# Second block of a two-block model: gate steps moved, a pair of selection products, denominators over a sum of tiles, a pair of output tiles

## What is computed

```python
h = rms_norm_2(x, norm1_g)
z = h @ w_in + b_in                       # all branches' features and 4 x 1024 gates
# mLSTM, 4 heads of width 128; chunked in the reference, equal to the full causal form:
#   s_qk = (q k^T) * exp(decay[t, s] - m_t), causal
#   num = s_qk @ v ; den = sum over s of s_qk
#   h = num / max(|den|, exp(-m_t))
y_ml = rms_norm_2(mlstm(q, k, v, i, f), ml_norm_g) * sigmoid(mo)
y_fx = forgetting_attention(...)
# RG-LRU: r, i = sigmoid(block-diagonal products of xc)
#   a = exp(-8 r softplus(-lambda)); u = sqrt(1 - a^2) * (i * xc)
#   scan over time: h = a h + u ; y = h * gelu(ry)
y_lru = rg_lru_branch(...)
y_gla = gla(...)
ycat = stack([y_ml, y_fx, y_lru, y_gla])
yb = einsum('bsnw,nwd->bsnd', ycat, w_branch)
merged = sum(sigmoid(gates) * yb)
x = x + merged @ w_o
x = x + square(relu(rms_norm_2(x, norm2_g) @ w_up)) @ w_down
```

## Time and profile before

| | |
|---|---|
| median of 3 runs | 3535.67 us |
| the profiled execution, its own time | 3532.56 us |
| its span | 3530.8 us |
| TensorE busy | 97% of the span, 16646 matmul records |
| VectorE, ScalarE, GpSimd busy | 51%, 34%, 8% |
| TensorE's share of the chain that ended last | 92% |
| mean granted TensorE clock | 0.983 of full |

### The profile page before, as it was taken

The page is one execution under the profiler, slowest core; times in us unless marked ns, Lnnn a source line. Parts: engine busy times, 40 slices in busy tenths (PEclk is TensorE's granted clock), DMA queues, the critical chain, the costliest instruction groups (busy, mean ns, idle before and its releaser), DMA issues.

```text
span 3530.8 us, 40839 instructions
## 1 busy us (share of the span) xinstructions
PE 3435.0 (97%) x16646; PEld 2758.3 (78%) x16646; DVE 1786.8 (51%) x3100; ACT 1185.1 (34%) x1990; POOL 287.3 (8%) x238
## 2 busy tenths in 40 slices
PE   8999999999999999999899999999999999999999
PEld 6888786777888788887777878887788777878887
DVE  7666456565565733334654643334453655454433
ACT  3222236542222232223555332223321444223322
POOL 0000220002000200021200100013011000020000
PEclk9999999999999999999999999999999999999999
DMA  6565322123565523223210322322221223122232
GB/s 239 206 211 189 101 78 72 40 69 109 191 219 196 179 98 99 92 95 107 68 49 25 114 83 84 108 82 93 68 78 55 75 73 115 42 96 84 96 107 78
DMA packets 120218, 376.37 MB, mean 107 GB/s; under 512 B 13280, under 2 KB 28000, under 8 KB 120032
## 3 DMA queue, kind: packets, MB, share of 16 engines
q1 hardware_dynamic: 120032, 373.76, 31.8%
HBM read 371.61 MB, written 2.10 MB: 106 GB/s over the span
## 4 chain that ended last, share of the span: by engine, by line
PE 92%; DVE 4%; ACT 2%; issue 1%; POOL 1%; DMA 0%; SPq 0%; POOLq 0%; ACTq 0%; DVEq 0%
PE ps L445 26%; PE ps L446 26%; PE ps L447 26%; PE ps L660 2%; PE ps L683 2%; PE ps L554 2%; PE ps L488 1%; PE ps L495 1%; PE ps L479 1%; PE ps L481 1%; PE ps L480 1%; DVE s_wl L1429 1%; ACT s_wh L944 1%; POOL s_small L2109 0%; PE ps L521 0%
## 5 line engine op out<-in xcount | busy, mean ns | idle before, releaser
L445 PE MATMUL ps<-s_uh,s_wh 128*128 128x512 f32 x2824 | 1137.4, 403 | 30.2 <-DVE s_ul L1491 12.8
L1429 DVE TENSOR_TENSOR s_wl<-s_raw,s_wh 128x1024 fp32r<-128x1024 f32 (+3 forms) x645 | 707.1, 1097 | 845.2 <-ACT s_wh L944 843.0
L446 PE MATMUL ps<-s_uh,s_wl 128*128 128x512 f32 x2824 | 1111.1, 393 | 0.0
L447 PE MATMUL ps<-s_ul,s_wh 128*128 128x512 f32 x2824 | 1110.5, 393 | 0.0
L944 ACT ACTIVATE s_wh<-s_raw 128x1024 fp32r<-128x1024 f32 (+3 forms) x645 | 587.9, 913 | 727.6 <-PE ps L447 531.2
L445 PEld LDWEIGHTS ps<-s_uh,s_wh 128*128 128x128 f32 x2824 | 537.5, 190 | 173.1 <-issue 49.4
L447 PEld LDWEIGHTS ps<-s_ul,s_wh 128*128 128x128 f32 x2824 | 536.6, 190 | 115.1
L446 PEld LDWEIGHTS ps<-s_uh,s_wl 128*128 128x128 f32 x2824 | 537.9, 190 | 109.0 <-issue 2.4
L447 PE MATMUL ps<-s_fl,s_wh 128*128 128x512 f32 x960 | 378.2, 394 | 0.0
L445 PE MATMUL ps<-s_fh,s_wh 128*128 128x512 f32 x960 | 378.2, 394 | 0.0
L446 PE MATMUL ps<-s_fh,s_wl 128*128 128x512 f32 x960 | 378.2, 394 | 0.0
(11 more groups left out here) (401 smaller groups left out, 3374.1 us busy)
## 6 DMA issues: line engine op xcount, KB each, us to landing
s_raw<-w SPq DMA_DIRECT2D x616, 512.0 KB, 3.6
s_raw<-w SPq DMA_DIRECT2D x96, 192.0 KB, 2.4
s_raw<-w SPq DMA_DIRECT2D x64, 256.0 KB, 2.6
s_raw<-w SPq DMA_DIRECT2D x19, 128.0 KB, 2.0
s_x<-x SPq DMA_DIRECT2D x4, 512.0 KB, 6.3
out<-s_x SPq DMA_DIRECT2D x8, 256.0 KB, 2.2
s_raw<-w SPq DMA_DIRECT2D x4, 420.0 KB, 3.6
s_crow<-crow SPq DMA_DIRECT2D x2, 512.0 KB, 3.4
```

The lines of the kernel that those rows point to most:

```text
L445: TE.matmul(o, w_hi(i, k), h, start=first, stop=False)
L446: TE.matmul(o, w_lo(i, k), h, start=False, stop=False)
L447: return TE.matmul(o, w_hi(i, k), l, start=False, stop=last)
L1429: V.tensor_tensor(wl[w][:, 0:n], raw[t % NRAW][:, 0:n], wh[w][:, 0:n].bitcast(F32), SUB).then_inc(*s_lo.up(("lo", t)))
```

## The change

- mLSTM: four gate steps stand ahead of the transposes; the loop and `head_norm` keep theirs, so none is left for `merge(0)`.
- mLSTM: `lfm` lies at partitions 32 to 35, so that its selection product uses other rows of the array than that of `lmx`; both waits stand ahead of both products.
- mLSTM: the ones-product runs over the first 128 columns of `lE[0]`, and once over `lsum`, 384 columns, into which VectorE adds the four tiles. TensorE waits for the last addition; ScalarE waits for the additions before it overwrites `lE`; VectorE waits for the last `db` before it overwrites `lsum`.
- RG-LRU: two gate steps stand ahead of the products `ga` and `gx`; `merge(2)` has two fewer.
- Output: the first two `wo2` tiles are made by `fm_pair`.

```diff
@@ plan
-    for m in range(8):
+    pair("wo2", 0, "wo2", 1)
+    for m in range(2, 8):
         fm("wo2", 8, m)
@@ buffers
-            lai, lmx, lfm = (sb(d, n, [4, 512]) for n in ("lai", "lmx", "lfm"))
+            lai, lmx = (sb(d, n, [4, 512]) for n in ("lai", "lmx"))
+            lfm = sb(d, "lfm", [36, 512])[32:36, :]
+            lsum = sb(d, "lsum", [128, 384])
@@ tensor_engine, second
             c = Clock(0)
+            fill(c, 4)
             o = take(("acol",))
...
-                sel = col("sel", 128 * h, 128)[0:4, :]
+                sel = col("sel", 128 * h, 128)
                 mb, eb = take(("mb", h)), take(("eb", h))
                 pe.wait_ge(*s_dve["mx"])
-                TE.matmul(mb[:], sel, lmx[:], start=True, stop=True).then_inc(*s_pe.up(("ps", ("mb", h))))
                 pe.wait_ge(*s_dve["fmx"])
-                TE.matmul(eb[:], sel, lfm[:], start=True, stop=True).then_inc(*s_pe.up(("ps", ("eb", h))))
+                TE.matmul(mb[:], sel[0:4, :], lmx[:], start=True, stop=True).then_inc(*s_pe.up(("ps", ("mb", h))))
+                TE.matmul(eb[:], sel[32:36, :], lfm, start=True, stop=True).then_inc(*s_pe.up(("ps", ("eb", h))))
...
-                    TE.matmul(nb[:, 128 * j:512], lv[:, j, sl(h)], lE[j][:, 0:n], start=j == 0, stop=j == 3)
-                    TE.matmul(db[:, 128 * j:512], ones, lE[j][:, 0:n], start=j == 0, stop=j == 3).then_inc(
-                        *s_pe.up(("lE", h, j), *([("ps", ("nb", h)), ("ps", ("db", h))] if j == 3 else [])))
+                    ins = TE.matmul(nb[:, 128 * j:512], lv[:, j, sl(h)], lE[j][:, 0:n], start=j == 0, stop=j == 3)
+                    if j == 0:
+                        ins = TE.matmul(db[:, 0:128], ones, lE[0][:, 0:128], start=True, stop=True)
+                    ins.then_inc(*s_pe.up(("lE", h, j), *([("ps", ("nb", h))] if j == 3 else [])))
+                pe.wait_ge(*s_dve["lsum", h, 3])
+                TE.matmul(db[:, 128:512], ones, lsum[:], start=True, stop=True).then_inc(*s_pe.up(("ps", ("db", h))))
...
             c = Clock(2)
+            fill(c, 2)
...
-            for m in range(8):
+            fm_pair(("wo", "s", 0), "wo2", 0, ("wo", "s", 1), "wo2", 1, ("mu",))
+            for m in range(2, 8):
@@ scalar_engine, second
             c = Clock(0)
+            fill(c, 4)
...
                     if h:
                         act.wait_ge(*s_pe["lE", h - 1, j])
+                        act.wait_ge(*s_dve["lsum", h - 1, max(j, 1)])
...
             c = Clock(2)
+            fill(c, 2)
...
+            fm_pair("wo2", 0, "wo2", 1)
+            for m in range(2, 8):
@@ vector_engine, second
             V.tensor_tensor(lfm[:], lmx[:], ffx[0:4, :], ADD).then_inc(*s_dve.up("fmx"))
+            fill(c, 4)
             dve.wait_ge(*s_pe["ps", ("acol",)])
...
                     V.scalar_tensor_tensor(lE[j][:, 0:n], bank(g)[:, 0:n], 128.0 ** -0.5, lE[j][:, 0:n], MUL, MUL).then_inc(*s_dve.up(("mE", h, j), frees=g))
+                    if j:
+                        if j == 1 and h:
+                            dve.wait_ge(*s_pe["ps", ("db", h - 1)])
+                        dve.wait_ge(*s_dve.now())
+                        o = 128 * j - 128
+                        first = lE[0][:, 128:512] if j == 1 else lsum[:, o:384]
+                        V.tensor_tensor(lsum[:, o:384], first, lE[j][:, 0:n], ADD).then_inc(*s_dve.up(("lsum", h, j)))
...
             c = Clock(2)
+            step(c, 2)
...
+            fm_pair("wo2", 0, "wo2", 1)
             for m in range(8):
-                fm("wo2", 8, m)
+                if m > 1:
+                    fm("wo2", 8, m)
                 dve.wait_ge(*s_pool["fx", m])
                 update(("wo", "s", m), m, None, ("x", "up", m))
```

## The result

Over 20 runs each on the same chips, the changed kernel took 3532.98 us in the median (3525.47 to 3540.83) and the kernel before 3537.88 (3532.71 to 3542.83). The ratio is 0.9979, 95% interval 0.9972 to 0.9987: 7.4 us less, with 4.6 to 9.9 as bounds (the two medians alone are 4.9 apart). The forecast was 8.6 us less. The forecast of 3527.1 us was counted from a median of 3535.67; this series has the kernel before 2.2 us higher, and 3532.98 as such lies 1 us above the range.

A forecast was written before the change was run, and what follows sets the result against it. The prediction took TensorE, busy 97% of the span, to bound the kernel. Its terms -3.9 + 1.1 - 3.4 - 5.3 + 0.2 + 0.2 + 2.5 made -8.6 us, forecast 3527.1 us, range 3522 to 3532.

The forecast's parts named there:

- mLSTM, four steps: Start of mLSTM: waits of 2.24 us and half clock go, -3.9 us; at its end a br0 wait, +1.1.
- The clock part, -1.6: mLSTM head 0: the 1.62 us it takes longer than head 1 is half clock and goes with the waits.
- Selection pair: mLSTM heads: two selection products overlap on two row groups, 1.06 us for 1.92, -3.4 us for four heads.
- the second rival: mLSTM: the two selection products don't overlap; total -5.2 us, 3530.5 us; chance 0.1.
- Denominators: mLSTM heads: 768 of 1280 columns go, 1.32 us a head, -5.3 us for four; sum ready with 1.2 us slack.
- the third: mLSTM: GpSimd holds head 3's additions and the tail also halves the clock; total -6.2 us, 3529.5 us; chance 0.12.
- the fourth rival: mLSTM: TensorE waits for the sum in every head, 9.0 us for four; slower, 3536.1 us; chance 0.04.
- The +0.2 for head 3: mLSTM head 3: additions held beside GpSimd's squarings make the sum late; bounds 0 and +0.9 us, +0.2 taken.
- RG-LRU: RG-LRU gate tiles: the 2.94 us wait goes, one of 3.8 us comes later; bounds -0.7 and +1.0, +0.2 us taken.
- Output pair: First wo2 tiles: one wait of about 5.4 us for VectorE's split, half clock behind it; +2.5 us.
- The clock terms: Half clock behind waits: 1.62 us gone in mLSTM, 1.7 to 2.9 lost in RG-LRU and at the output pair.
- The first rival: RG-LRU and output pair: the clock does not fall behind the two new waits; total -11.7 us, 3524.0 us; chance 0.15.

The follow-up runs named there:

- steps_only: The kernel before with only the four gate steps ahead of the mLSTM head loop; 3541.61 us, ratio 1.0014 to before.
- ml_only: The changed kernel without the output pair and the two RG-LRU steps, so the three mLSTM edits together; 3528.08 us, ratio 0.9979 to before.
- no_pair: The changed kernel with the first output tiles made one after the other again; 3524.52 us, ratio 0.9969 to before.
- lru_tanh: The changed kernel with ScalarE's RG-LRU order turned: three gate steps' work before the first branch-tile copy, four behind each; 3523.30 us, ratio 0.9954 to before.
- den_only: The kernel before with only the denominators taken over the added tiles; 3532.90 us, ratio 0.9991 to before.
- best_alone: The changed kernel without the output pair, with lru_tanh's ScalarE order and three gate steps ahead of the mLSTM heads; 3519.01 us, ratio 0.9948 to before.
- best_pair: best_alone with the output pair, its second weight tile split ahead of merged tile 6; 3517.87 us, ratio 0.9948 to before.
- best_dense: best_alone with eight gate steps among gla's four heads in place of four; 3516.17 us, ratio 0.9938 to before.
- sel_only: The kernel before with only the selection products on two row groups; 3533.45 us, ratio 0.9989 to before.

## Why the prediction was right, and where it was not

The total came out near its forecast (7.4 us less for 8.6). Of the mechanisms the waits and the overlap were right but for one tanh in RG-LRU and one bank in mLSTM; the clock was not, and that the total fits all the same is in part luck (the sum, below).

- **mLSTM, four steps.** Right in the waits (2.24 us gone, none new at the start) and in the tail (+1.1 forecast; a wait of 0.80). The clock part, -1.6, was taken as if half clock needed a wait ahead. It went in all ten profiles with the three edits, but steps_only kept it without any wait, so filling the waits was not enough. Behind the heads, where the changed kernel has 3.4 us of it as before, ml_only, no_pair and lru_tanh have 6.8.
- **Selection pair.** The pair took 1.05 us where 1.06 was forecast, so the second rival fell. The term was too large all the same, 0.84 once and then 0.59 a head for 0.86: of a head's length the text looked at TensorE's products and at the wait for the sum, not at the bank of the third score product, which hangs on VectorE's reciprocal of the head before.
- **Denominators.** 1.29 to 1.32 us for 1.32 a head; additions of 0.56, 0.42 and 0.29 for 0.55, 0.42 and 0.29; slack 1.5 us for 1.2. In head 3 the additions took the same 0.56, 0.42 and 0.29, and no head waited at the sum, so neither the third nor the fourth rival came. But this was the timing, not a missing conflict: the squarings had just ended. In den_only they held two additions by 0.91 us together, the forecast's "up to 0.9", and the slack took it; in best_alone, best_pair and best_dense the additions of 384 and 256 columns took 0.81 each, and the sum was ready 0.06 us before TensorE asked. The +0.2 for head 3 was right in size by luck: 0.25 us were lost at its first numerator, not at the sum.
- **RG-LRU.** Wrong in one step: "The first goes", and "the next tanh that TensorE needs, of tile 4". TensorE needs the tanh of tile 3 earlier, to start tile 5. Of 2.94 us 1.18 stayed, because ScalarE's tanh of tile 3 stands behind the first copy, and the first tanh after the square roots pays for a load of the table, 1.28 us. The load was in the trace of before, too, and was not counted. The Trainium skill (ScalarE: Activation LUTs, "What ACT_TABLE_LOAD costs") gives 1283 ns for it, as the row here, and a drain of about 1.4 us besides, of which this row shows nothing: the load starts 0.02 us behind the copy, and the tanh 0.02 us behind the load. The second wait came where it was forecast (3.49 us for 3.8), the third (0.88) went, and the stage cost 0.9 us, inside the bounds of -0.7 and +1.0 and above the +0.2 taken. The two steps were not run alone, but no_pair is ml_only with them: 78.2 us for 80.1, so some 2 of the 2.7 moved away, as in the changed kernel.
- **Output pair.** Right by the profiles: start of the pair, wait (5.30 for 5.4), its releaser, the half clock behind it. The stage cost 2.1 for 2.5, and 0.7 more came in the part behind it, where all six profiles of the changed kernel and its variants with the pair show 10.4 to 10.8 us of half clock, and six of the eight without it 6.9 to 7.5.
- **The sum.** Without the clock the terms make -2.24 + 1.1 - 3.4 - 5.3 + 0.2 - 0.7 + 0.3 = -10.0 us; the runs, with each one's half clock taken off, show -9.9. That this agrees so closely is luck: the pair of products gave less than 3.4, RG-LRU cost 0.9 for a gain of 0.7 at full clock, and the two spans, with half of their half clock taken off, differ by 8.2. The clock terms were +1.5 together; by the mean clocks they should have been 4 to 6, by the ratio of the first series about 2.5. The step that failed is that the clock was reckoned only at the waits that the change touches: in the changed kernel's profile the 17.1 us among gla's heads lie behind none of them. The first rival (the clock does not fall) fell, too.

What stays open: why a gla stage with the same instructions is granted half clock for 3 us in one execution and for 17 or 31 in another, and whether the mLSTM steps make the long form more frequent, as six of eleven profiles with them against none of three without suggest (over 10 us of half clock there). So few profiles can fall out like this by chance, about once in six. Where the stretch starts says more: in seven profiles the clock first fell 2.5 to 3.6 us behind the first state product, and five of them have over 10 us; in the other seven it fell 15 us behind it or later, and one has. Denser heads did not settle it.

## What to carry to other kernels

Before moving work into a wait, look in each other engine's own order for what stands ahead of the releasing instruction: here 4.7 us of waits and 3.4 of slower clock fell to one reordering on ScalarE, more than any one edit of the change gave. A saving per loop turn is worth only what the chain of the turn before leaves, so check when each bank or buffer of the next turn comes free. And where a profile's total moves against the edits, cut both timelines at the same instructions and set the half clock of each piece beside it, over several executions, before believing either.

## What the runs showed of the hardware

TensorE ran at 1.2 GHz while it was busy without a gap: 17.10 of 17.10 us, 64 matmuls, where 17 us from the same place in the kernel before held 112. No wait stood ahead of it; the engine had run products of 128 columns or fewer since its last gate step; and the same instructions ran mostly at 2.4 GHz in another execution (no_pair, 6.8 us at half for 17.1). The Trainium skill (TensorE: Matmul & The Clock Gate, "HAM oscillation — how this bites in real kernels") tells of falls behind waits for DMA; here none was waited for. In RG-LRU, on the other hand, half clock cost nothing where other engines set the pace: that stage took 80.2 us with 6.8 us of it and 80.1 us with none (sel_only).

VectorE's operations were longer beside GpSimd's squarings: 2.06 us for a split of weights that takes some 1.3 alone, 1.18 for a scaling of 0.42, 0.81 for additions of 0.42 and 0.29. The array took two fp32 products of 4 rows, on rows 0 to 3 and 32 to 35 and into two banks, at once: 1.05 us for both, 1.92 on the same rows one after the other.
